# The scale group of the first conditioning is made on VectorE from transposed weights, beside the shift group on TensorE

## The reference

```python
sc  = jax.nn.silu(c)         # [1, 1024]
scc = jax.nn.silu(c_ctx)     # [1024]
m  = (sc  @ ada_w[0] + ada_b[0]).reshape(-1, 9, 1024)   # 9 groups for the latent tokens
mc = (scc @ ada_w[0] + ada_b[0]).reshape(9, 1024)       # 9 groups for the context tokens
# group 0 is the shift, group 1 the scale of the first norm, group 2 its gate, ...
x = x + 0.5 * m[:, 2] * swiglu(rmsnorm(x, g) * (1 + m[:, 1]) + m[:, 0], wg, wu, wd)
h = h + 0.5 * mc[2]   * swiglu(rmsnorm(h, g) * (1 + mc[1])   + mc[0],   wg, wu, wd)
# then a state-space mixer, three more feed-forward layers, a pooling mixer, and
# a second block of attention and a product-key expert layer (two layers)
```

## Time and profile before

| | |
|---|---|
| median of 3 runs | 3246.74 us (3244.81 to 3247.67) |
| the profiled execution | 3242.28 us |
| its span, first to last instruction | 3240.4 us |
| TensorE busy over the span | 81% |
| VectorE busy over the span | 68% |
| TensorE busy in the first 400 us | 382.7 us |

### The profile page before, as it was taken

The page is one execution under the profiler, slowest core; times in us unless marked ns, Lnnn a source line. Parts: engine busy times, 40 slices in busy tenths (PEclk is TensorE's granted clock), DMA queues, the critical chain, the costliest instruction groups (busy, mean ns, idle before and its releaser), DMA issues.

```text
span 3240.4 us, 37121 instructions
## 1 busy us (share of the span) xinstructions
PE 2631.2 (81%) x13830; PEld 1983.2 (61%) x13830; DVE 2218.0 (68%) x3855; ACT 1019.2 (31%) x2144; POOL 738.4 (23%) x679
## 2 busy tenths in 40 slices
PE   8999998897699989689874688768876778775666
PEld 5999986686589989689764445225542446321122
DVE  3886866737537868758616666986679775987755
ACT  3433322112233343333322342233322343221222
POOL 0000000003200000000000233443434433445543
PEclk9999998999899999899887889889888889887799
DMA  7766942240058859549545799999999999999998
GB/s 285 267 236 264 366 177 95 94 143 25 20 200 325 357 207 355 196 171 356 220 148 225 318 406 420 421 421 412 421 420 420 396 409 419 421 421 420 419 422 335
DMA packets 136868, 976.51 MB, mean 301 GB/s; under 512 B 15501, under 2 KB 15509, under 8 KB 18976
## 3 DMA queue, kind: packets, MB, share of 16 engines
q0 software_dynamic: 90512, 656.51, 49.8%
q1 hardware_dynamic: 45072, 312.26, 25.3%
q10 hardware_dynamic: 1152, 6.04, 0.5%
HBM read 973.69 MB, written 1.06 MB: 301 GB/s over the span
## 4 chain that ended last, share of the span: by engine, by line
PE 48%; DMA 27%; DVE 15%; ACT 5%; issue 5%; POOL 1%; DVEq 0%; ACTq 0%; POOLq 0%
PE psum L610 48%; DMA rows<-in_peer,eidx 26%; DVE arena L1424 2%; DVE yacc L1427 2%; DVE arena L1560 1%; DVE wlow L1424 1%; DVE rows L2111 1%; PE psum L613 1%; ACT L1046 1%; DVE arena L1430 1%; DVE arena L1427 1%; ACT u L1046 1%; DMA wring<-in_keys 1%; POOL rows L2238 0%; ACT dots L1046 0%
## 5 line engine op out<-in xcount | busy, mean ns | idle before, releaser
L610 PE MATMUL psum<-rows,diag 128*128 128x512 f32 x1392 | 784.1, 706 | 390.8 <-ACT diag L1046 384.3
L2111 DVE CUSTOM_DVE_ANT_0 rows<-rows,h2tok 128x1024 f32<-128x1024 f32 x512 | 626.1, 1225 | 367.4 <-DMA rows<-in_peer,eidx 360.0
L2238 POOL DMA_INDIRECT rows<-in_peer,eidx x512 | 624.7, 1220 | 975.4 <-PE psum L610 556.5
L610 PEld LDWEIGHTS psum<-rows,diag 128*128 128x128 f32 x1392 | 285.1, 218 | 817.6 <-ACT diag L1046 539.7
L610 PE MATMUL psum<-u_hi,whigh 128*128 128x256 f32 x1760 | 504.3, 287 | 17.7 <-DVE u_lo L1427 14.1
L610 PE MATMUL psum<-u_lo,whigh 128*128 128x256 f32 x1760 | 501.0, 285 | 0.0
L610 PE MATMUL psum<-u_hi,wlow 128*128 128x256 f32 x1760 | 500.8, 285 | 0.0
L1424 DVE TENSOR_TENSOR wlow<-wring,whigh 128x2048 fp32r<-128x2048 f32 x165 | 376.9, 2288 | 161.3 <-ACT whigh L1046 155.1
L1046 ACT ACTIVATE whigh<-wring 128x2048 fp32r<-128x2048 f32 x165 | 314.0, 1908 | 206.8 <-PE psum L610 133.8
L610 PEld LDWEIGHTS psum<-u_hi,whigh 128*128 128x128 f32 x1760 | 340.5, 193 | 21.2 <-issue 15.0
L610 PEld LDWEIGHTS psum<-u_lo,whigh 128*128 128x128 f32 x1760 | 341.1, 194 | 0.0
(11 more groups left out here) (265 smaller groups left out, 3234.3 us busy)
## 6 DMA issues: line engine op xcount, KB each, us to landing
arena<-in_ada_t POOLq DMA_DIRECT2D x112, 1024.0 KB, 7.0
wring<-in_ffn_w_gate SPq DMA_DIRECT2D x55, 1024.0 KB, 6.0
wring<-in_ffn_w_up SPq DMA_DIRECT2D x55, 1024.0 KB, 6.4
wring<-in_ffn_w_down SPq DMA_DIRECT2D x55, 1024.0 KB, 6.5
wring<-in_w_in SPq DMA_DIRECT2D x32, 1024.0 KB, 9.1
wring<-in_peer_wq SPq DMA_DIRECT2D x32, 1024.0 KB, 9.1
wring<-in_ssd_w_in SPq DMA_DIRECT2D x30, 1024.0 KB, 4.8
wring<-in_w_out SPq DMA_DIRECT2D x16, 1024.0 KB, 9.1
```

The costliest lines, as they stand in the source:

```text
L610: return nc.tensor.matmul(out, lhsT, rhs, start=start, stop=stop, skip_group_check=shared)
L2111: v.tensor_tensor_reduce(out=rows[:, n % SLOTS, 0:D], in0=rows[:, n % SLOTS, 0:D], in1=h2tok[:, t, :], scale=1.0, scalar=0.0, op0=ALU.mult ...
L2238: pool.indirect_dma_start(out=rows[:, n % SLOTS, :], out_offset=None, in_=A[f"peer{u // 2}"], in_offset=bass.IndirectOffsetOnAxis(ap=eidx[ ...
```

## The change

The second half of `ada_w0` is no longer loaded or multiplied on TensorE. In its place GpSimd's queue loads four chunks of `ada_t` (the same 4 MB of weights, transposed), the first three at once at the start of the program and the fourth when VectorE has done with the first. VectorE makes the scale group from them in `scale_first`, with sixteen multiply-and-sum instructions over 1024 elements. For that it needs the rows of `c` and `c_ctx` on all partitions and through Silu, so ScalarE's queue loads two rows of `crow` (1 MB) ahead of `hT`, and ScalarE waits for them and puts them through Silu ahead of `squares(0)`.

```
-STAGES = [("ada0", 8), ...
+STAGES = [("ada0", 4), ...
 # SP
-            for group in range(2):
-                for i in range(4):
-                    load(A["ada_w0"][4 * group + i])
+            for i in range(4):
+                load(A["ada_w0"][i])
 # TensorE: norm_sums(0), first_rows(), then ffn(0)
+            def first_rows():
+                for i in range(4):
+                    w = tile().rearrange("p (k n) -> p k n", k=2)
+                    for k in range(2):
+                        for half in range(2):
+                            ins = mm(psum[0:2, half, :], silu_c[:, 2 * i + k, 0:2], ...
+                    ins.then_inc(weights_consumed, 1)
+                    if i == 1:
+                        pe.wait_ge(std_ready, 1)
+                        norm_sums(1)
+                pe.wait_ge(arow_ready, 1)
+                for b in range(KB):
+                    ins = transpose(bank(6, b * 2, 2), arow[:, 0, b * P:(b + 1) * P])
+                ins.then_inc(arow_turned, 1)
 # VectorE: scale_first(), mods_first(), norm(0), low(0, 1), low(0, 2), ffn(0)
+            def scale_first():
+                dve.wait_ge(crow_ready, 1)
+                for i in range(ADA_TURNS):
+                    if i == 3:
+                        dve.wait_ge(std_ready, 1)
+                        tick(v.reciprocal(rstd[:], std[:]))
+                    dve.wait_ge(ada_in[i % ADA_RING], 16 * (i // ADA_RING + 1))
+                    if i:
+                        dve.wait_ge(ada_step, ADA_FREE + i)
+                    for j in range(2):
+                        w = aring[:, i % ADA_RING, j, :]
+                        c = KB + 2 * i + j
+                        v.tensor_tensor_reduce(out=spare[:, j, :], in0=w, in1=crow[:, 1, :], ... accum_out=modsc[:, c:c + 1])
+                        ins = v.tensor_tensor_reduce(out=w, in0=w, in1=crow[:, 0, :], ... accum_out=mods[:, c:c + 1])
+                    ins.then_inc(ada_step, 1)
+            def mods_first():
+                dve.wait_ge(weights_consumed, consumed("ada0", 3))
+                dve.wait_ge(ada_step, ADA_BASE[0])
+                v.tensor_copy(arow[:, 0, :], psum[0:2, 0:2, :]...).then_inc(arow_ready, 1)
+                for m in (mods, modsc):
+                    tick(tt(m[:, KB:2 * KB], m[:, KB:2 * KB], col("ada_b", KB, KB), ALU.add))
+                settle()
+                tick(stt(gscale[:, 0, :], NORMS[0][3], 1.0, NORMS[0][1], ALU.add, ALU.mult))
+                low(0, 0)
+                dve.wait_ge(arow_turned, 1)
+                ...
 # GpSimd
+            def scale_chunk(i):
+                if i >= ADA_RING:
+                    pool.wait_ge(ada_step, ADA_FREE + i - ADA_RING + 1)
+                pool.dma_start(aring[:, i % ADA_RING]..., A["ada_t"][4 + i]).then_inc(ada_in[i % ADA_RING], 16)
+            for i in range(ADA_RING):
+                scale_chunk(i)
```

More of the change, by code:

```diff
@@ L81 @@
 ADA_TURNS = 4
-ADA_BASE = [ADA_FREE + ADA_TURNS * sum(count for _, count, _ in ADA[:n]) for n in range(len(ADA) + 1)]
+ADA_BASE = [ADA_FREE + ADA_TURNS + ADA_TURNS * sum(count for _, count, _ in ADA[:n]) for n in range(len(ADA) + 1)]
 COLS = {}
@@ L613, in transpose @@
                 return nc.tensor.transpose(out, in_, ident[0:in_.shape[0], 0:in_.shape[0]])
[L615 to L628, removed]
+            def first_rows():
[3 more added lines that the diff above has]
+                        for half in range(2):
+                            ins = mm(psum[0:2, half, :], silu_c[:, 2 * i + k, 0:2], w[:, k, half * 512:(half + 1) * 512],
+                                     i == 0 and k == 0, i == 3 and k == 1)
+                    ins.then_inc(weights_consumed, 1)
[5 more added lines that the diff above has]
+                    ins = transpose(bank(6, b * 2, 2), arow[:, 0, b * P:(b + 1) * P])
                 ins.then_inc(arow_turned, 1)
@@ L1048, in _ @@
             act.dma_start(xT[:], A["xT"]).then_inc(x_in, 16)
+            act.dma_start(crow[:, 0:2], A["c_rows"][0:2].unsqueeze(0).to_broadcast([P, 2, D])).then_inc(crow_in, 16)
             act.dma_start(hT[:], A["hT"]).then_inc(h_in_sem, 16)
@@ L1055, in _ @@
             f(silu_c[:, :, 2], col("c2", 0, 8), ACT.Silu).then_inc(silu_c_ready, 1)
-            f(exp_a[:], cols[0:64, COLS["a_log"][0]:COLS["a_log"][0] + 1], ACT.Exp).then_inc(act_step, 1)
+            act.wait_ge(crow_in, 16)
+            f(crow[:, 0:2], crow[:, 0:2], ACT.Silu).then_inc(crow_ready, 1)
             def squares(n):
@@ L1147, in _ @@
             squares(0)
+            deviation(0)
             squares(1)
-            act.dma_start(crow, A["c_rows"].unsqueeze(0).to_broadcast([P, 3, D])).then_inc(crow_in, 16)
-            deviation(0)
+            f(exp_a[:], cols[0:64, COLS["a_log"][0]:COLS["a_log"][0] + 1], ACT.Exp).then_inc(act_step, 1)
             for t in range(HIGH_RING):
@@ L1154, in _ @@
             deviation(1)
-            act.wait_ge(crow_in, 16)
-            f(crow, crow, ACT.Silu).then_inc(crow_ready, 1)
             ffn(0)
@@ L1438, in _ @@
             v.memset(hgate[0:1, 0, 0:1], 0.0).then_inc(ada_step, ADA_FREE)
[L1440 to L1449, removed]
+            def scale_first():
[10 more added lines that the diff above has]
+                        c = KB + 2 * i + j
+                        v.tensor_tensor_reduce(out=spare[:, j, :], in0=w, in1=crow[:, 1, :], scale=1.0, scalar=0.0,
+                                               op0=ALU.mult, op1=ALU.add, accum_out=modsc[:, c:c + 1])
+                        ins = v.tensor_tensor_reduce(out=w, in0=w, in1=crow[:, 0, :], scale=1.0, scalar=0.0,
+                                                     op0=ALU.mult, op1=ALU.add, accum_out=mods[:, c:c + 1])
+                    ins.then_inc(ada_step, 1)
@@ L1493, in norm @@
                     return
-                scaled(n)
+                if n:
+                    scaled(n)
                 if n == 3:
@@ L1547, in ffn @@
                 dve.wait_ge(crow_ready, 1 if n < 2 else 2)
-                uses = [ADA_TURNS * sum(ADA[m][1] > a for m in range(n)) for a in range(7)]
+                uses = [(2, 1, 1, 0, 0, 0, 0)[a] + ADA_TURNS * sum(ADA[m][1] > a for m in range(n)) for a in range(7)]
                 def condition(a, it):
@@ L1598, in _ @@
             dve.wait_ge(cols_in, 16)
-            for t in range(3):
-                low(0, t)
-            mods_first((0, 1), 1)
+            scale_first()
+            mods_first()
             norm(0)
+            low(0, 1)
+            low(0, 2)
             ffn(0)
@@ L2302 @@
         "xT": blocks(I["x"]), "hT": blocks(I["ctx"]), "cols": np.ascontiguousarray(cols),
-        "ada_w0": tiles(I["ada_w"][0][:, 0:2 * D], 2, D), "c_rows": np.concatenate([I["c"].reshape(1, D), I["c_ctx"].reshape(1, D), I["c_2"].reshape(1, D)]),
+        "ada_w0": tiles(I["ada_w"][0][:, 0:D], 2, D), "c_rows": np.concatenate([I["c"].reshape(1, D), I["c_ctx"].reshape(1, D), I["c_2"].reshape(1, D)]),
         "ada_t": tiles(ada_rows, 2, D),
```

17 lines of the change are left out of this document (12 added, 5 removed).

## The result

The changed kernel takes 3237.86 us in the median of 14 runs (3234.24 to 3242.05), the kernel before 3245.97 us beside it (14 runs, 3242.79 to 3248.69). The ratio is 0.9974 with a 95% interval of 0.9966 to 0.9981: 8.4 us faster, between 6 and 11. The span of the profiled execution is 3235.0 us against 3240.4.

What follows compares the result with a forecast made beforehand. The prologue's path to layer 0 was taken to bound the kernel: `u` at 46.3 against 52.18, 5.9 us earlier, less 0.8 for the clock, gives 5.1, so 3246.74 - 5.1 = 3241.6 us. Range 3236.5 to 3246.5.

Steps and rivals of the forecast that it cites:

- What bounds the prologue: Prologue before layer 0: TensorE's products and VectorE's `wlow` end together; whatever moves layer 0's start moves the end equally.
- t: Landing of `crow` on ScalarE's queue, from which everything starts: 15.9 us, between ends of 12.0 and 19.6.
- the head start that I gave the others: In the landing of `crow`: about 1.2 us off equal turns, as GpSimd's transfers are set up last.
- From t to the end of the products: Prologue: Silu, squares, first sums, products, second sums, products on ScalarE and TensorE; 26.2 us, ending at 42.1.
- From the copy to `u`: Prologue's tail: one copy, two adds and `gscale`, one `wlow`, two adds and waits; 4.2 us, `u` at 46.3.
- The clock: Start of layer 0: TensorE's granted clock may fall after idling; 0.8 us lost, between nothing and 2.0.
- Sum: Whole kernel: 5.9 us earlier `u` less 0.8 for the clock, a gain of 5.1 us.
- the bound of "faster": Whole kernel's time: a gain over 0.2% (6.5 us) counts as faster; chance 0.29.
- an early `crow`: Rival, prologue: GpSimd's queue gets nothing in before `crow`, which lands at 12.0; gain 9.0 us, 3237.7; chance 0.28.

Runs made afterwards that it cites:

- e7: Changed kernel with GpSimd issuing its chunks only once `crow` has landed, and its masks first; ratio 0.9983 to the kernel before.
- e1: Changed kernel with `crow` loaded behind `hT` instead of ahead of it in ScalarE's queue; ratio 0.9996 to the kernel before.
- the repeat: Changed kernel run and profiled once more, unaltered; ratio 0.9972 to the kernel before.
- e10: Changed kernel with host array `ada_w0` kept at its old 8 MB, second half never read; ratio 0.9971 to the kernel before.
- e2: Kernel before with only VectorE's order changed: one `wlow` and the reciprocal ahead of the copies, two `wlow` later; ratio 0.9983.
- e6: Changed kernel with second sums behind the transposes and the issues of `xT` and `crow` exchanged; ratio 0.9962 to the kernel before.
- e9: Kernel before with VectorE's order changed as in e2 and the shift group's row copied early; ratio 0.9983.
- e8: As e6, with `hT` also issued only behind `deviation(0)`; ratio 0.9962 to the kernel before.
- e3: Changed kernel with all three `wlow` ahead of the copy again; ratio 0.9973 to the kernel before.
- e5: Changed kernel with ScalarE's `squares(0)` ahead of its wait for `crow` and the Silu; ratio 0.9961 to the kernel before.
- e4: Changed kernel with TensorE's second sums behind the transposes again, not among the products; ratios 0.9957 and, once more, 0.9961 to the kernel before.

## Why the prediction was right, point by point

**What bounds the prologue** was read rightly: the mark moved with `u` in every kernel, and the layers behind follow it. In e1 7.2 us put into `u` were 7.3 us of the mark.

**t.** Forecast 15.9; measured 15.2, 14.7 and about 15.1. The working holds: without GpSimd's queue 12.2 (e7), with it 3.0 us more, where I had 3.9, and three even turns, to be seen in the changed kernel from 8 to 9 us (packets, MB, share):

```profile
q1 hardware_dynamic: 18, 0.15, 34.8%
q10 hardware_dynamic: 17, 0.14, 32.8%
q0 software_dynamic: 16, 0.13, 30.9%
```

GpSimd's first packets came only between 5 and 6 us; the head start that I gave the others was right in kind, but is 1.9 us and not 1.2. The Trainium skill ("DMA: Bandwidth & Descriptors", section on queues, rings and completion order) has the engines go round their queues packet by packet, with about a dozen descriptors to a packet. The trace agrees with the going round, 18 to 17 to 16 rows of 8 KB in one microsecond; with 13 to 13 rows in the 0.3 us from 3.9 on it fits turns of single rows better than turns of a dozen.

**From t to the end of the products.** Forecast 26.2, measured 25.3 (15.17 to 40.43), 26.1 in the repeat and 26.7 or so in e10. The second sums were 3.7 us as read from the warm group, and the first sums scatter from 5.1 to 6.6. The terms were right within that scatter. (The working's "started 9.8 us later" should read 9.7 by its own rows; nothing hangs on it.)

**From the copy to `u`.** Forecast 4.2, measured 3.95 in all three profiles.

**The clock.** Forecast 0.8; from `u` to the mark are 10.0 us in the kernel before, in e2 to e6 and in e9, 10.5 in e1, e7 and e8 (in e8 because its second sums, 6.45 us long, held the layer's start), and 10.48, 10.87 and 11.10 in the changed kernel's three profiles: 0.5 to 1.1. A layer 0 that begins at 0.50 is not enough for a loss, though. It did so in e3 and e5 too, at no cost:

```profile
44.00:46.00 2.00, 2.00 (x10) 0.50 1.00 418
46.00:48.00 2.00, 1.91 (x11) 0.78 0.22 82
```

These are rows of e5, with `u` at 41.78. The last three blocks of `u_lo` start 5.2 us behind `u` in each of these kernels. In e5 and e3 the granted clock was back at 1.00 5.1 and 5.3 us behind `u`, in the changed kernel's three profiles 6.9, 7.8 and 8.4. So the slower passes were hidden as long as TensorE had to wait for blocks, which is what the prediction had said of the first five, and only what was still slow behind the last block was paid.

**Sum.** Forecast 5.1 us earlier. The mark moved by 7.3, 6.5 and 5.4 in three profiles of the same instructions, 6.4 in the mean. The mechanism was right and the sum 1.3 us short: 0.9 of it is t, and 0.2 each the way to the end of the products and the way from the copy to `u`. That the span of the profile, 3235.0, lies beside the forecast 3235.3 is luck: there the mark had moved by 7.3 and the span by 5.4.

**The time moved more than the mark.** 8.4, 9.1 and 9.4 us in three comparisons, so it lies above the 6.5 us at which I had put the bound of "faster", where the chance was 0.29. The time stayed within the range because its lower end was made for an early `crow`, and not because a term allowed for more than the prologue gave. One to four us of the gain, 2.6 in the mean of the three, are not in the mark. An extra stands in all eleven comparisons of kernels with the sum on VectorE (the time less the movement of the mark is 1.1 to 4.0 us, 2.6 in the mean; e1, whose mark didn't move, has 1.3), and not in the two with order changes alone (e2 5.5 us at a mark of 5.9, e9 5.5 at 6.4). Each of these has an uncertainty of some 3 us, and they are not independent: all marks are counted from the one profile of the kernel before. I looked in three places. In layer 0, at a wait of 2.3 us for `wlow` near 127 us, the granted clock fell to 0.53 for some microseconds in the kernel before and stayed at 1.00 in the changed one:

```profile
127.00:129.00 2.00, 1.18 (x10) 1.00 0.77 303
129.00:131.00 2.00, 2.00 (x12) 0.53 1.05 442
131.00:133.00 2.00, 2.00 (x14) 0.62 0.67 279
```

```profile
119.70:121.70 2.00, 1.16 (x9) 1.00 0.85 324
121.70:123.70 2.00, 2.00 (x19) 1.00 0.99 418
```

That is worth 1.5 us (twelve of SP's loads later the marks are 8.8 apart, not 7.3), but it happened in some profiles of either kind and not in others: in the second and third profile of the changed kernel and in e2, not in e4 and e9. The place of the tables in memory is made unlikely by e10 (0.9971), not ruled out. The later stages scatter by 4 us from one execution to the next: three profiles of the changed kernel's instructions, with marks at most 1.9 apart, end at 3235.0, 3236.2 and 3240.8. What the extra is, or whether it is there, stays open.

**What brought the gain.** Most of it needed no work moved to VectorE. The order alone gave 5.9 us of the mark, with the first copy taken early 6.4, and the changed kernel had 6.4 in the mean; of the time, either gave 5.5 us of the 8.4. The change halved TensorE's products (13.7 us), and gave it nearly all back by waiting for `crow` (8.8 us later start) and by taking the second sums in between (3.7 us). Only with one of these two undone (e4, e5) is the moved group worth its place: the mark at 51.8 to 52.2.

## What to carry to other kernels

When work is halved on one engine, look at what the rest of its queue now starts behind: here a wait for one transfer in front of the squares, needed by VectorE alone, held TensorE for 9 us. Before work is moved to another engine, take everything off the tail that has time elsewhere (a reciprocal, two of three roundings, an early copy), and measure that alone. And a group that is off the path belongs into the idle time, not between the products on the path: that alone was 2.5 us of `u` (e4). Whether it also helps by bringing the clock back isn't shown, since e5, without it, reaches the same mark.

## What was not expected of the hardware

- The same 16 records on a TensorE that had not yet run took 5.1 to 6.6 us, while the record of the granted clock says 1.00 throughout. Their weight loads took 338 ns and late 190 ns. The same loads took up to 338 ns in the second sums of the kernel before, at a granted 0.50, and 190 ns in those of the changed kernel, at 1.00. So the loads point to the lower level at the start, where the record doesn't.
- GpSimd's queue, issued at 1.35 us, moved its first packet after 5 us, some three microseconds after the other two queues; a chunk issued at 12.9 among full queues (e7) landed after 10.4 us.
- A fall of the granted clock after an idle stretch comes or doesn't for the same stretch of the same program: after 2.3 us of waiting it fell to 0.50 in the second profile of the changed kernel and stayed at 1.00 in the first.
